# Products of zeros in TensorE's pauses, and an expert's first seven weight slabs asked for during the routing

## What is computed

```python
def moe_swiglu(h, router, wg, wu, wd):
    logits = (h @ router).astype(jnp.float32)
    top_v, top_i = lax.top_k(logits, TOP_K)
    gates = jax.nn.softmax(top_v, axis=-1)
    combine = jnp.sum(jax.nn.one_hot(top_i, N_EXPERTS, dtype=jnp.float32) * gates[..., None], axis=-2)
    for e in range(N_EXPERTS):
        y = y + combine[..., e:e + 1] * swiglu(h, wg[e], wu[e], wd[e])
...
    for i in range(DEPTH):
        hn = rmsnorm_2(h, ln_mix[i])
        (aq, ak, av, hy, gq, gk, gv, go, glr, gates) = split_cols(hn @ w_in[i], IN_SPLITS)
        y_a = attention_mixer(aq, ak, av, attn_qnorm[i], attn_knorm[i], cos, sin) @ w_br_attn[i]
...
        y_b = hyena_mixer(hy, hy_conv[i], spec, hy_skip[i]) @ w_br_hyena[i]
        y_c = gla_mixer(gq, gk, gv, go, glr, gla_w_lr[i], gla_b_lr[i], gla_onorm[i]) @ w_br_gla[i]
        gate = jax.nn.sigmoid(gates.reshape(B, L, N_BRANCH, D_MODEL))
        mixed = gate[:, :, 0] * y_a + gate[:, :, 1] * y_b + gate[:, :, 2] * y_c
        h = h + mixed @ w_out[i]
        h = h + memory_cross_attention(rmsnorm_2(h, ln_x[i]), rmsnorm_2(mem, ln_mem[i]),
                                       x_wq[i], x_wk[i], x_wv[i], x_wo[i], x_qnorm[i], x_knorm[i])
        hn = rmsnorm_2(h, ln_mlp[i])
        h = h + jnp.square(jax.nn.relu(hn @ mlp_w1[i])) @ mlp_w2[i]
```

## Time and profile before

| what | us |
|---|---|
| median of three runs | 3038.49 |
| the runs | 3040.75, 3023.25, 3038.49 |
| the profiled execution | 3035.28 |
| its span in the trace | 3033.5 |
| TensorE busy | 2845.3 (94%) |
| VectorE busy | 2004.4 (66%) |
| ScalarE busy | 1513.7 (50%) |
| mean granted clock of TensorE | 0.953 |

### The profile page before, as it was taken

One profiled execution on the slowest core, in us unless ns is written; L12 is line 12 of the kernel. 1 busy time (PEld: TensorE's weight loads), 2 busy tenths in 40 slices (PEclk: granted clock), 3 DMA queues, 4 the chain that ended last, 5 costly groups with the idle time before them and its releaser, 6 DMA issues. The chain is left out here.

```text
span 3033.5 us, 43342 instructions
## 1 busy us (share of the span) xinstructions
PE 2845.3 (94%) x17693; PEld 2528.4 (83%) x17693; DVE 2004.4 (66%) x2003; ACT 1513.7 (50%) x1456; POOL 68.8 (2%) x55
## 2 busy tenths in 40 slices
PE   5999998699999999999997989999899899999999
PEld 5799997588888888888885767999899777989898
DVE  6555564488888888888884555565555565665554
ACT  3443353367667776677762425444433326343442
POOL 1000000000000000000000110000000110000000
PEclk8899987699999999999997999999999999999999
DMA  6255540199999999999994332444355433444353
GB/s 185 70 172 188 170 153 16 65 366 335 374 334 356 353 334 376 333 355 352 334 376 147 132 98 91 146 153 142 102 187 183 131 116 107 140 141 138 126 186 105
DMA packets 365123, 619.38 MB, mean 204 GB/s; under 512 B 14664, under 2 KB 201126, under 8 KB 363700
## 3 DMA queue, kind: packets, MB, share of 16 engines
q1 hardware_dynamic: 363432, 611.77, 58.5%
q10 hardware_dynamic: 1550, 5.57, 0.5%
HBM read 611.93 MB, written 5.37 MB: 203 GB/s over the span
## 5 line engine op out<-in xcount | busy, mean ns | idle before, releaser
L354 DVE TENSOR_TENSOR slots_low<-slots,w_hi 128x2048 fp32r<-128x2048 f32 x240 | 549.4, 2292 | 397.6 <-ACT w_hi L343 397.5
L343 ACT ACTIVATE w_hi<-slots 128x2048 fp32r<-128x2048 f32 x240 | 452.0, 1887 | 367.7 <-PE ps L925 188.1
L1251 DVE TENSOR_TENSOR slots_low<-slots,w_hi 128x2048 fp32r<-128x2048 f32 x224 | 504.0, 2285 | 65.4 <-ACT w_hi L1202 65.4
L456 PE MATMUL ps<-x_hi,w_hi 128*128 128x256 f32 x1520 | 449.0, 295 | 53.2 <-DVE x_lo L536 26.7
L456 PE MATMUL ps<-x_lo,w_hi 128*128 128x256 f32 x1520 | 442.3, 291 | 0.0
L456 PE MATMUL ps<-x_hi,slots_low 128*128 128x256 f32 x1520 | 441.9, 291 | 0.0
L1202 ACT ACTIVATE w_hi<-slots 128x2048 fp32r<-128x2048 f32 x224 | 415.9, 1908 | 1.6 <-DMA slots<-in_moe_w_up_dram 1.5
L456 PEld LDWEIGHTS ps<-x_hi,w_hi 128*128 128x128 f32 x1520 | 304.8, 201 | 61.4 <-issue 54.4
L1135 PE MATMUL ps<-slots_low,x_hi 128*128 128x512 f32 x896 | 350.0, 391 | 0.0
L456 PEld LDWEIGHTS ps<-x_lo,w_hi 128*128 128x128 f32 x1520 | 305.1, 201 | 0.3
L456 PEld LDWEIGHTS ps<-x_hi,slots_low 128*128 128x128 f32 x1520 | 304.3, 200 | 0.0
(11 more groups left out here) (536 smaller groups left out, 5367.2 us busy)
## 6 DMA issues: line engine op xcount, KB each, us to landing
slots<-in_moe_w_gate_dram SPq DMA_DIRECT2D x112, 1024.0 KB, 5.1
slots<-in_moe_w_up_dram SPq DMA_DIRECT2D x112, 1024.0 KB, 5.1
slots<-in_moe_w_down_dram SPq DMA_DIRECT2D x112, 1024.0 KB, 4.9
slots<-in_mlp_w_dram SPq DMA_DIRECT2D x64, 1024.0 KB, 5.2
slots<-in_w_in_dram SPq DMA_DIRECT2D x54, 1024.0 KB, 5.3
slots<-in_ffn_w_gate_dram SPq DMA_DIRECT2D x14, 1024.0 KB, 5.0
slots<-in_ffn_w_up_dram SPq DMA_DIRECT2D x14, 1024.0 KB, 5.0
slots<-in_ffn_w_down_dram SPq DMA_DIRECT2D x14, 1024.0 KB, 4.9
```

Of the source, the lines that this page charges most:

```text
L343: act.activation(w_hi[:, s.buffer, 0:s.kt * s.cols], slots[:, s.slot, 0:s.kt * s.cols], ACT.Copy).then_inc(w_hi_done, 1)
L354: dve.tensor_tensor(slots_low[:, s.slot, 0:n], slots[:, s.slot, 0:n], w_hi[:, s.buffer, 0:n].bitcast(F32), ALU.subtract).then_inc(w_lo_don ...
L456: mm = pe.matmul(b[:, t * T:(t + 1) * T], w, xx[:, k, :], **flags)
L1251: dve.tensor_tensor(low[i % NS], raw[i % NS], his[i % R].bitcast(F32), ALU.subtract).then_inc(lo_done, 1)
```

## The change

`keep_busy` gets the bank as an argument, and is called at five more kinds of place: 12 products ahead of each attention's first turn, before its wait (five calls), 24 between the mLSTM's last products and its transposes, 50 at the end of the opening on TensorE, 16 at the end of each hyena, 16 at the last item of each linear with side work. That is 198 products in a program that had 40.

In `experts`, the first seven loads of expert 0 are issued by SyncE before the stage begins, behind a wait for the last use of the slab before (the mLSTM's out weights). The 35 other slabs of expert 0 are written out, without a register in their addresses, and the number of passes is loaded behind them; the loop then starts at pass 1.

```diff
-    def moe_stage(*names):
+    def moe_stage(begin, *names):
         sems = [nc.alloc_semaphore(name=f"{n}_moe", num=SEM0 + 45 + k) for k, n in enumerate(names)]
+        begin(sems)
         with nc.Block() as block:
             yield (block, *sems)
...
-        def keep_busy(pe, n):
+        def keep_busy(pe, n, b=7):
             for _ in range(2 * n):
-                pe.matmul(bank(7)[:, 0:T], zeros[:, 0:P], zeros[:, :], start=True, stop=True)
+                pe.matmul(bank(b)[:, 0:T], zeros[:, 0:P], zeros[:, :], start=True, stop=True)
...
                     def turn(j):
+                        if j == 0:
+                            keep_busy(pe, 6)
                         pe.wait_ge(weighted, j + 1)
...
+            def load(sp, sem, weights, i):
+                kind, g, n = plan[i]
+                if kind == "first":
+                    src = weights[n // 2][:, n % 2 * KH:(n % 2 + 1) * KH, g * W:(g + 1) * W]
+                else:
+                    src = weights[2][:, 4 * g + 2 * n:4 * g + 2 * n + 2, :]
+                sp.dma_start(slots[:, i % NS, :].rearrange("p (k n) -> p k n", k=src.shape[1]), src).then_inc(sem, 16)
+
+            first_pass = [w[:, 0] for w in (gate, up, down)]
+
+            def first_loads(sems):
+                nc.sync.wait_ge(w_used, stream.slabs[after - 1].used_after)
+                for i in range(NS):
+                    load(nc.sync, sems[i], first_pass, i)
...
-                    sp.wait_ge(used, NS)
-                    n = passes(sp, body)
+                    for i in range(NS, SLABS):
+                        sp.wait_ge(used, i + 1)
+                        load(sp, landed[i % NS], first_pass, i)
+                    n = sp.value_load(jobs[0:1, NJOB:NJOB + 1], min_val=NE, max_val=NJOB - 1)
+                    with sp.Fori(1, n) as j:
+                        body(j)
...
                         mm.then_inc(turned, 1)
+                    keep_busy(pe, 25, 1)
...
                                     mm.then_inc(back, 1)
+                    keep_busy(pe, 8, 0)
...
-                                ("dve", 6): side_invert, ("pe", 6): both(logits, side_spread), ("dve", 7): both(lower, side_keys), ("act", 7): softplus, ("dve", 8): log_decay})
+                                ("dve", 6): side_invert, ("pe", 6): both(logits, side_spread), ("pe", len(items) - 1): lambda pe, more: keep_busy(pe, 8), ("dve", 7): both(lower, side_keys), ("act", 7): softplus, ("dve", 8): log_decay})
...
+                            keep_busy(pe, 12)
                             for h in range(NH):
                                 pe.wait_ge(scaled, (2 * h + 1) // 3 + 1)
```

More of the change, by code:

```diff
@@ L1042, in experts @@
             at = {slab: i for i, slab in enumerate(plan)}
-            with ExitStack() as c, moe_stage(*[f"landed{s}" for s in range(NS)], "used", "hi_done", "lo_done", "src_hi_done", "src_lo_done",
+            def load(sp, sem, weights, i):
[10 more added lines that the diff above has]
+                    load(nc.sync, sems[i], first_pass, i)
+            with ExitStack() as c, moe_stage(first_loads, *[f"landed{s}" for s in range(NS)], "used", "hi_done", "lo_done", "src_hi_done", "src_lo_done",
                                          "activated", "hidden", "turned", "turned_hi", "turned_lo", "act_out", "dve_out",
@@ L1070, in body @@
                         e = sp.value_load(jobs[0:1, bass.ds(j, 1)], min_val=0, max_val=NE - 1)
-                        gw, uw, dw = (w[:, bass.ds(e, 1)].rearrange("p e k n -> p (e k) n") for w in (gate, up, down))
-                        for i, (kind, g, n) in enumerate(plan):
+                        weights = [w[:, bass.ds(e, 1)].rearrange("p e k n -> p (e k) n") for w in (gate, up, down)]
+                        for i in range(SLABS):
                             sp.wait_ge(used, SLABS * j + i + 1)
-                            if kind == "first":
-                                src = (gw, uw)[n // 2][:, n % 2 * KH:(n % 2 + 1) * KH, g * W:(g + 1) * W]
-                            else:
-                                src = dw[:, 4 * g + 2 * n:4 * g + 2 * n + 2, :]
-                            sp.dma_start(raw[i % NS].rearrange("p (k n) -> p k n", k=src.shape[1]), src).then_inc(landed[i % NS], 16)
-                    sp.wait_ge(used, NS)
-                    n = passes(sp, body)
+                            load(sp, landed[i % NS], weights, i)
+                    for i in range(NS, SLABS):
[4 more added lines that the diff above has]
+                        body(j)
                     for s in range(AHEAD):
```

## The result

The changed kernel's median is 3017.31 us over 13 runs, that of the kernel before 3039.73 over 13 (3023.25 to 3048.35). Twelve of the changed kernel's runs lie between 3009.66 and 3033.78 (their median is 3016.20); the thirteenth took 10218.62 us, for a reason that nothing here shows, and is in no comparison. The ratio is 0.9947, 95% interval 0.9928 to 0.9965, so 11 to 22 us faster, 0.5%; the medians differ by 22.4 us, the upper end of that. The forecast was 3030, within 1% of before. The profiled execution of the changed kernel took 3012.16 us (span 3010.3), 23.1 less than that of before.

The account below looks back on a forecast made before the run. TensorE, busy 94% of the span, was taken to bound the kernel. Terms −0.2, −1.3, −5.0, −1.6 and +2.6, the rest 0, gave −5.5 us from the profiled 3035.3: 3029.8, said as 3030, range 3012 to 3044.

Parts of the forecast that it names:

- Early slabs: Experts' start: seven slabs loaded early save at most the 0.4 us of idle issue; −0.2 us, ends 0 and −0.4.
- DMA-paced rival: Expert stage: DMA sets the pace after all, so seven slabs in hand are worth 19 us; 3011 in all, chance 0.04.
- Loads beside the routing: Routing before the experts: seven megabytes of loads slow its small operations, +1 to +2 us, part of the range only.
- MLA: MLA attention's first turn: 12 products before ready work cost 2.6 us, or raise the clock earlier; 0, ends −1.7 and +2.6.
- mLSTM: Before the mLSTM's transposes: 24 products fall into a 4.31 us wait for VectorE; 0, ends 0 and +0.8 us.
- Opening: Opening's end: 50 products leave 4.3 us of a 9.70 us pause idle, the clock falls; 0, ends −8.4 and +1.0.
- the clock's hold as a rival: Opening's end: the clock holds into the spectra, a further −8.4 us, giving 3021; chance 0.15.
- Linear's 16: Linear before each eight-head attention: 16 products fit the 2.75 us pause; nothing by themselves, but help keep the clock.
- Hyena's end: Each hyena's end: 16 products keep the clock; −1.3 us at layer 0 (ends 0 and −1.7), 0 at layer 1.
- Eight-head attention: Eight-head attentions: 12 products per layer fill the first turn's wait and the clock holds; −5.0 and −1.6 us.
- Cross: Cross attentions' first turns: 12 products each before ready work cost 1.3 us each, +2.6 us; ends 0 and +2.6.

Follow-up runs that it names:

- run 3: The changed kernel without the 12 products in MLA's attention and the 24 in the mLSTM, early loads kept; ratio to the kernel before 0.9920, median 3015.49 us.
- run 6: The changed kernel without the 16 products at the end of each linear with side work; ratio to the kernel before 0.9945, median 3016.10 us.
- run 9: The changed kernel without the 16 products at each hyena's end; ratio to the kernel before 0.9948, median 3018.20 us.
- run 1: The changed kernel without its 198 products, only expert 0's early loads left; ratio to the kernel before 0.9987, median 3036.46 us.
- run 8: Changed kernel without MLA, mLSTM and cross products, 84 at the opening: 0.9916 of before, 3008.59 us; the same with the cross's 12 put back: 0.9926, 3012.40 us.
- the lean version: The changed kernel without products in MLA, mLSTM and cross attentions, with 84 at the opening's end; ratio to the kernel before 0.9916, median 3008.59 us.

## Why the prediction was right, and where it wasn't

The time (3017.3) lay in the range of 3012 to 3044 and on the forecast side, and "within 1%" was right. The size was not: the sum had 5.5 us to gain, and 11 to 22 were measured. The low ends together gave 3019 and would not have held 3017; what held it are the microseconds put below that for the spread of the runs. (That sum took the cross attentions at +2.6. With their own low end of 0 it is −19.0, and 3016.) By its steps:

- *Early slabs, −0.2, ends 0 and −0.4.* Right, at the end 0: 0.42 us of "issue" stayed, so even those weren't the slab's. The DMA-paced rival is out: seven slabs asked for 58 us ahead of the first product changed no wait. Loads beside the routing cost it nothing that shows: from the router's first product to the experts' first gather it is 37.1 us with them, 37.1 with the zeros alone and 38.1 before.
- *MLA, +2.6 against an earlier rise, taken as 0.* Right for this trace: the twelve took 2.54 us at half clock (89.72 to 92.26), and the 2.8 us by which the first turn came later were made up by 95.8. It was too cautious in the mean: over all traces the stage is 2.2 us shorter with the twelve (run 3), by the earlier rise that I named and gave nothing.
- *mLSTM, 0.* Right for the 24: they sit at 494.70 to 497.4, the pause behind shrank to 1.73 us. I did not see that the whole stage can run at either clock, 24.6 or 33.4 us.
- *Opening, 0, with the clock's hold as a rival.* Right: 4.23 us of idleness left, I said 4.3, and the clock fell. The rival's size was right too, once 84 products close the pause: 9.1 where I bounded 8.4. What the Trainium skill states of transposes ("TensorE: Matmul & The Clock Gate", Part 4, on PE-mode transpose), that they don't count as busy in the same way, pointed to a clock that outlasts the fifty; with fifty behind the transposes the window was 0.53 as against 0.51, so the trace gives it no support here, and what mattered was the idleness left.
- *Linear's 16, nothing by themselves.* Right, and nearly nothing with the others: 0 and 0.3 us (run 6). My reason for the eight-head gain, "both falls lie behind the two idle times", named one pause too many.
- *Hyena's end, −1.3 and 0.* Right against the trace that they were read from (66.4 to 65.2 us, and 65.2 both times), too small for the kernel: −2.7 at layer 0 (run 9), and in run 1's trace layer 1 has 2.7 to lose too.
- *Eight-head attention, −5.0 and −1.6.* Right against the trace that they were read from (−4.7 and −1.3), too small for the kernel. In the trace of the loads alone the attentions take 29.8 us each, so the same products are worth 12.1 us there, not 6.6. This is the term that was mis-sized.
- *Cross, +2.6.* Wrong, and for its reason, "with nothing behind to save". The price is 1.1 us each, and the linear behind, at half clock in its first microseconds without the products (0.76 and 0.78 over 7 us), is 1.4 us shorter in eleven of sixteen places (run 8). The two together come to about zero.
- *Not in the sum:* layer 1's first linear, 2.9 us shorter than in before's trace (45.2 to 42.3), where the change put nothing. Part of the 10.9 us of the second block is thus luck of this pair of traces; whether the products make the shorter time likelier is open.

The step that failed is the choice named in the second paragraph: "Sums are made against the profiled execution". I noted that this execution lies 3.2 us below the median but did not ask in which stretches. Layer 1's attention was read at 0.89, and I took this for its state rather than for one draw; the 17.5 us between the three runs said that the half-clock stretches are draws, and I used them only to widen the range. A usual second block of before is about 11 us longer than the one that I read from (1395.7 by the sum in run 3, 1396.6 in run 1, against 1384.4), and this is most of the way from 3030 to 3017. From run 1's trace to the changed kernel's the block is 23.0 us shorter: 12.1 in the eight-head attentions, 5.4 in the linears behind the hyenas, 3.6 in layer 1's first linear and hyena, 1.6 in the linears behind the cross attentions, 2.5 in other stretches, less 2.2 that the cross attentions cost.

## What to carry to other kernels

When runs of one kernel spread by more than the change should bring, a stretch whose clock reads low in one place and high in its twin (layer 0 and layer 1) can be a draw: take a second trace, and size the gain with the worse of the two in view, since what a filled pause buys is that the worse one doesn't happen. Fill a pause of TensorE down to about a microsecond of idleness: fifty products in 9.7 us left 4.23 and bought nothing, 84 left 0.52 and bought 9 us. Ask first whether TensorE is what the work behind waits for: at the spectra's end the clock was held and VectorE kept the time. In front of ready work the products cost their 0.11 us each (0.21 at half clock), and may still earn it back at the next pause, as in the cross attentions and MLA; read the stage behind before leaving them out, as the lean version did.

## What the runs showed of the hardware that I had not expected

- In the same stretch, with the same code before it, TensorE's clock is 1.00 in one execution and near 0.5 in another (the mLSTM's first 12 us: 0.59 in before, 1.00 with the loads alone), so a single trace can be 8.8 us off in one stage (33.4 against 24.6).
- The changed second block came out alike in four traces: 1373.54, 1373.40, 1373.40 and 1373.53 us in kernels that differ elsewhere, as against 1384.4 and 1396.6 without the products. Part of that is chance: in one of the four the spectra took 1.6 us more and the linear behind the first cross attention 1.4 less. Nor need it be so in each execution: the changed kernel's twelve times spread over 24 us, the first block's stretch in all traces over 16.
- A pause of 2.20 us was enough: with the twelve left out and no longer one inside the attention, layer 1's eight heads took 28.22 us against 23.75.
- A gain at one place can come with a fall at another: with 84 products the spectra gained 9.1 us, and the trace's second block ended where it was, as 2.4 us were lost in layer 0's hyena and 6.2 in layer 1's first linear and hyena; in the lean version the same 84 kept theirs.
